# Two model blocks on one core: the first products of each wide norm on unscaled input, latent norms earlier

## What is computed

```
def rmsnorm(x, g):
    xf = x.astype(jnp.float32)
    y = xf * lax.rsqrt(jnp.mean(xf * xf, axis=-1, keepdims=True) + EPS)
    return (y * g.astype(jnp.float32)).astype(x.dtype)

# block 1
hn = rmsnorm(h, mix_norm_g[l]);  proj = hn @ w_in[l]
q_a, k_a, v_a, cq, ckv, k_pe = jnp.split(proj, IN_SPLITS, axis=-1)
#   q, k, v: windowed attention, 8 heads; cq, ckv (512 and 256 columns) are
#   normed again ("latent norms") and go through w_q_up and w_kv_up
h = h + mix @ w_out[l]
h = h + conv_glu(rmsnorm(h, ffn_norm_g[l]), w_gate[l], w_up[l], ...)
#   conv_glu: (silu(conv3(x @ w_gate)) * (x @ w_up)) @ w_down

# block 2; mod = silu(c) @ w_ada + b_ada gives shift, scale and gate of both norms
h = rmsnorm_2(x, norm_mix_g[l]) * (1.0 + sc_m) + sh_m;  proj = h @ w_in[l]
#   a recurrence (hgrn) and a convolution, gated sum "merged"
x = x + gt_m * (merged @ w_o[l])
h2 = rmsnorm_2(x, norm_ffn_g[l]) * (1.0 + sc_f) + sh_f
ff = (silu(h2 @ w_ffn_gate[l]) * (h2 @ w_ffn_up[l])) @ w_ffn_down[l]
x = x + gt_f * ff;  return rmsnorm_2(x, norm_final_g)
```

## Time and profile before

| | before |
|---|---|
| median of 3 runs | 2782.65 us (2779.78 to 2783.17) |
| the profiled execution | 2776.33 us, span 2775.0 us |
| mean granted clock of TensorE | 0.985 of full speed |
| PE busy / DVE busy / ACT busy / POOL busy | 97% / 65% / 44% / 12% of the span |
| moved by DMA | 571 MB, mean 206 GB/s |

### The profile page before, as it was taken

How to read it: one execution, slowest core, us unless ns; L and a number is a source line. 1 busy time by engine, 2 the same in 40 slices (tenths; PEclk the granted TensorE clock), 3 DMA queues, 4 the chain that set the end, 5 groups by cost and what they waited for, 6 DMA issues and landing times. The chain is left out here.

```text
span 2775.0 us, 51102 instructions
## 1 busy us (share of the span) xinstructions
PE 2682.7 (97%) x22036; PEld 2638.7 (95%) x22036; DVE 1800.6 (65%) x2489; ACT 1214.8 (44%) x1861; POOL 321.6 (12%) x533
## 2 busy tenths in 40 slices
PE   7899989899999999998999999999899999999998
PEld 6888879899999999998999999999899999999997
DVE  5656567877777777775788667767554454444454
ACT  4456544544433444434444443334444443344442
POOL 1110113211111111221000001111100000000001
PEclk9999999999999999999999999999999999999999
DMA  6343457688888787885444568887545555555553
GB/s 198 119 118 91 125 178 230 216 266 272 271 280 284 267 274 267 273 275 175 152 152 148 180 224 275 270 278 244 166 164 186 188 181 184 194 192 187 182 186 118
DMA packets 500001, 571.18 MB, mean 206 GB/s; under 512 B 26688, under 2 KB 473280, under 8 KB 499776
## 3 DMA queue, kind: packets, MB, share of 16 engines
q1 hardware_dynamic: 467968, 463.76, 51.2%
q0 software_dynamic: 31520, 103.36, 11.4%
q10 hardware_dynamic: 288, 0.80, 0.1%
HBM read 565.77 MB, written 2.54 MB: 205 GB/s over the span
## 5 line engine op out<-in xcount | busy, mean ns | idle before, releaser
L1596 DVE TENSOR_TENSOR wl<-raw,wh 128x1024 fp32r<-128x1024 f32 (+1 forms) x894 | 1060.3, 1204 | 675.3 <-ACT wh L1143 669.8
L575 PE MATMUL ps<-xx,wh 128*128 128x256 f32 (+2 forms) x5104 | 1459.2, 286 | 39.3 <-DVE xx L1651 18.1
L576 PE MATMUL ps<-xx,wh 128*128 128x256 f32 (+2 forms) x5104 | 1439.1, 282 | 0.0
L577 PE MATMUL ps<-xx,wl 128*128 128x256 f32 (+2 forms) x5104 | 1435.7, 281 | 0.0
L1143 ACT ACTIVATE wh<-raw 128x1024 fp32r<-128x1024 f32 (+1 forms) x894 | 880.9, 1029 | 639.0 <-PE ps L577 631.3
L575 PEld LDWEIGHTS ps<-xx,wh 128*128 128x128 f32 x5104 | 967.2, 190 | 49.4 <-issue 30.2
L576 PEld LDWEIGHTS ps<-xx,wh 128*128 128x128 f32 x5104 | 968.4, 190 | 1.7 <-issue 1.0
L577 PEld LDWEIGHTS ps<-xx,wl 128*128 128x128 f32 x5104 | 967.7, 190 | 0.0
L575 PE MATMUL ps<-hid,wh 128*128 128x256 f32 x1408 | 394.0, 280 | 0.0
L576 PE MATMUL ps<-hid,wh 128*128 128x256 f32 x1408 | 393.6, 280 | 0.0
L577 PE MATMUL ps<-hid,wl 128*128 128x256 f32 x1408 | 392.8, 279 | 0.0
(11 more groups left out here) (300 smaller groups left out, 1949.4 us busy)
## 6 DMA issues: line engine op xcount, KB each, us to landing
raw<-in_w_in SPq DMA_DIRECT2D x118, 1024.0 KB, 5.2
ada_raw<-in_w_ada POOLq DMA_DIRECT2D x384, 256.0 KB, 4.8
raw<-in_w_gate SPq DMA_DIRECT2D x44, 1024.0 KB, 6.7
raw<-in_w_up SPq DMA_DIRECT2D x44, 1024.0 KB, 7.1
raw<-in_w_ffn_gate SPq DMA_DIRECT2D x44, 1024.0 KB, 5.0
raw<-in_w_ffn_up SPq DMA_DIRECT2D x44, 1024.0 KB, 5.1
raw<-in_w_down SPq DMA_DIRECT2D x32, 1024.0 KB, 6.7
raw<-in_w_ffn_down SPq DMA_DIRECT2D x32, 1024.0 KB, 5.5
```

Of the source, the lines that this page charges most:

```text
L575: pe.matmul(dst, h[:, c, o:o + w], x[:, 0, k, g.t0:g.t1], start=(k == 0), stop=False)
L576: pe.matmul(dst, h[:, c, o:o + w], x[:, 1, k, g.t0:g.t1], start=False, stop=False)
L577: m = pe.matmul(dst, l[:, c, o:o + w], x[:, 0, k, g.t0:g.t1], start=False, stop=end)
L1596: dve.tensor_tensor(wl[i % NS][:, part], raw[i % NR][:, part], wh[i % NS][:, part].bitcast(F32), ALU.subtract).then_inc(s_lo, 1)
```

## The change

Each wide norm (`N_IN`, `N_FFN1`, `N_MIX2`, `N_FFN2`) gets a raw operand: chunk times norm gain, without `rstd`, in two parts (ACT `raw_his`, DVE `raw_lows`), made two chunks behind the residuals of the products before. The first two products after the norm (`RAW_KEY`, `RAW_KEY2`) run on it (`gemm_raw`), with the sums of squares inside the first; `rstd` multiplies their results as they are read from PSUM (`unscaled`). The norm itself is a lane paced by ticks, for the third product on. In block 2 the shift is carried as two more columns of the product and added afterwards (`keep_shift`, `shift_of`). The hold is gone. `ada` pauses in these two products and from `merged` to the second `wo` product, and begins four steps later.

At the start SP loads the first part of `H`, slab 0, then the rest; the squares' sums of `N_IN` are POOL's alone; the constants come in two loads. The latent norms start one product earlier, beside `kpe`, and their steps are spread. In the final norm ACT multiplies by the gain beforehand, DVE multiplies 12 chunks in three instructions and POOL four.

```diff
+RAW_LAG = {N_FFN1: {g: ([2 * g - 2, 2 * g - 1] if g < 7 else [12, 13, 14, 15]) for g in range(1, 8)},
+           N_MIX2: {g: ([2 * g - 2, 2 * g - 1] if g < 7 else [12, 13, 14, 15]) for g in range(1, 8)},
+           N_FFN2: {5: [0, 1, 2, 3, 4, 5], 6: [6, 7, 8, 9, 10, 11], 7: [12, 13, 14, 15]}}
+SUMS_AT = {N_IN: 12, N_FFN1: 8, N_MIX2: 8, N_FFN2: 8}
+ROOT_AT = {N_IN: 7, N_FFN1: 5, N_MIX2: 5, N_FFN2: 5}
+SCALE_AT = {N_IN: 8, N_FFN1: 8, N_MIX2: 9, N_FFN2: 6}
 def sync_program(sp):
-            for i in range(4):
-                sp.dma_start(H[:, 4 * i:4 * i + 4, :], hT[:, 4 * i:4 * i + 4, :]).then_inc(s_h[i], 16)
-            sp.wait_ge(s_h[1], 16)
+            sp.dma_start(H[:, 0:4, :], hT[:, 0:4, :]).then_inc(s_h[0], 16)
+                if i == 0:
+                    for q in range(1, 4):
+                        sp.dma_start(H[:, 4 * q:4 * q + 4, :], hT[:, 4 * q:4 * q + 4, :]).then_inc(s_h[q], 16)
 def tensor_program(pe):
+            def gemm_raw(n, key, sums=None):
...
+                for i in g.slabs:
...
+                    for c in range(nk):
+                        k = k0 + c
...
+                        if sums is not None and k == SUMS_AT[n]:
+                            sums(n)
+                        pe.wait_ge(s_rl, raw_base(n) + k + 1)
...
+                        elif sums is None and k in RAW_SHARED[n]:
+                            m.then_inc(s_passed, 1)
+                        if c in ticks(nk):
+                            lanes.pump(c == nk - 1 or c == nk // 2 - 1)
-            pair_sums(N_IN)
-            x_in = normed(N_IN)
-            gemm(("cq", 0), x_in)
-            gemm(("cq", 1))
-            gemm(("ckv", 0))
+            gemm_raw(N_IN, ("cq", 0), pair_sums)
+            gemm_raw(N_IN, ("cq", 1))
+            gemm(("ckv", 0), normed(N_IN))
+            lanes.start("latent", latent())
             gemm(("kpe", 0))
-            lanes.start("latent", latent())
...
+                        if f == 0 and g == 0:
+                            lanes.stop("ada")
+                            gemm_raw(n, (b, "gate", f, g), square_sums)
+                            gemm_raw(n, (b, "up", f, g))
+                            lanes.resume("ada")
+                            continue
-            square_sums(N_FFN1)
             ffn(1)
-            square_sums(N_MIX2)
...
                 if len(gs) == 2:
+                    lanes.stop("ada")
                     lanes.start("merged", pause(12), slow=True, front=True)
...
-                gemm(("wo", g), merged_ready if g == 0 else None, hold=(g == 7))
+                gemm(("wo", g), merged_ready if g == 0 else None)
+                if g == 1:
+                    lanes.resume("ada")
 def gpsimd_program(pool):
+            def first_pairs():
+                bufs = pair_bufs(N_IN)
+                for i in range(KD // 2):
+                    c = norm_src(N_IN, 2 * i + 1)
+                    pool.wait_ge(s_h[(2 * i + 1) // 4], 16)
+                    pool.tensor_tensor(bufs[i][1][:, :], c, c, ALU.mult).then_inc(s_pm, 1)
+                    if i:
+                        add_pair(i - 1)
+                add_pair(KD // 2 - 1)
 def scalar_program(act):
+            def raw_his(n, chunks):
+                for i in chunks:
+                    act.activation(raw_body(n, 0, i), raw_src(n, i), ACT.Copy, scale=norm_gain(n, i)).then_inc(s_rh, 1)
...
                 for j in range(2):
                     squares(N_FFN1, 2 * g + j, H[:, 2 * g + j, 14:T], *last_use(("outa", g), j))
+                raw_his(N_FFN1, RAW_LAG[N_FFN1].get(g, []))
 def vector_program(dve):
+            def raw_lows(n, chunks):
+                for i in chunks:
+                    dve.wait_ge(s_rh, raw_base(n) + i + 1)
+                    dve.scalar_tensor_tensor(out=raw_body(n, 1, i), in0=raw_src(n, i), scalar=norm_gain(n, i), in1=raw_body(n, 0, i).bitcast(F32),
+                                             op0=ALU.mult, op1=ALU.subtract).then_inc(s_rl, 1)
...
-            split(halves[0] + 2)
-            reciprocal(N_FFN1)
-            emit(norm_scales(N_FFN1))
+            lanes.start("norm", norm_scales(N_FFN1), front=True)
             ffn(1)
...
-            for c in range(KD):
-                if c % 4 != 1:
-                    x = H[:, c, 16:T]
...
+            for q in range(3):
+                x = H[:, 4 * q:4 * q + 4, 16:T]
+                dve.wait_ge(s_fa, 4 * q + 4)
+                dve.tensor_tensor(x, x, rstd[:, 0:SEQ].unsqueeze(1).to_broadcast([P, 4, SEQ]), ALU.mult).then_inc(s_fd, 1)
```

More of the change, by code:

```diff
@@ L444, in done, with raw_half, raw_body, raw_src @@
             return GEMMS[key].done
+        def raw_half(n, h, i):
+            if n == N_IN:
+                return raw_in[:, h, i, :]
+            if n == N_FFN2:
+                return raw_ffn[:, h, i, :]
+            return xb[:, h, i, :] if n == N_FFN1 and i < 8 else xx[:, h, i, :]
+        def raw_body(n, h, i):
+            return raw_half(n, h, i)[:, RAW_T1[n] - (T - NORM_T0[n]):RAW_T1[n]]
+        def raw_src(n, i):
+            return H[:, i, NORM_T0[n]:T]
+        def raw_shift(n, h):
+            return xx[:, h, :, Q0:META] if n == N_MIX2 else raw_ffn[:, h, :, 0:META - Q0]
+        def shift_cols(n):
+            return mod[:, 0:16] if n == N_MIX2 else mod[:, 48:64]
+        def raw_base(n):
+            return KD * RAW_NORMS.index(n)
+        def shared_free(n, i):
+            g = GEMMS[RAW_KEY2[n]]
+            if i % 8 == 7:
+                return s_slab, g.slabs[i // 8] + 1
+            before = sum(len([c for c in RAW_SHARED[m] if c % 8 != 7]) for m in RAW_NORMS[:RAW_NORMS.index(n)])
+            return s_passed, before + len([c for c in RAW_SHARED[n] if c % 8 != 7 and c <= i])
+        def shift_of(j):
+            return small[:, 160 + j:161 + j]
         def last_use(key, j):
@@ L579, in gemm @@
                                 m.then_inc(s_slab, 1)
-                        if c in ticks(nk) and not (hold and last):
+                        if c in ticks(nk):
                             lanes.pump(c == nk - 1 or c == nk // 2 - 1)
@@ L799, in tensor_program @@
             for g in range(8):
-                gemm(("outa", g), normed(N_A) if g == 0 else None, hold=(g == 7))
+                gemm(("outa", g), normed(N_A) if g == 0 else None)
             def ffn(b):
@@ L1120, in gpsimd_program @@
                     mod_until(20)
-            emit(norm_lows(N_FFN2))
-            mod_until(24)
+            lanes.start("norm", norm_lows(N_FFN2), front=True)
             ffn(2)
-            for q in range(4):
-                x = H[:, 4 * q + 1, 16:T]
-                pool.wait_ge(s_rr, 9)
-                pool.wait_ge(*last_use((2, "down", 1, 2 * q), 1))
+            pool.wait_ge(s_rr, 9)
+            for c in range(12, KD):
+                x = H[:, c, 16:T]
+                pool.wait_ge(s_fa, c + 1)
                 pool.tensor_tensor(x, x, rstd[:, 0:SEQ], ALU.mult).then_inc(s_fp, 1)
@@ L1144, in split, with gemm @@
                     halves[0] += 1
-            def gemm(key, hold=False):
+            def gemm(key):
                 for i in GEMMS[key].slabs:
                     nk = SLABS[i][3]
-                    held = hold and i == GEMMS[key].slabs[-1]
-                    split(2 * (i + 1) if held else 2 * (i + 2) + 1)
+                    split(2 * (i + 2) + 1)
                     for c in range(nk):
-                        if held:
-                            continue
                         if c in ticks(nk):
@@ L1352, in scalar_program @@
             pair_squares(N_IN)
-            split(1)
             act.wait_ge(s_cst, 16)
-            root(N_IN)
-            emit(norm_his(N_IN, 0))
-            for g in range(2):
-                gemm(("cq", g))
-                for j in range(2):
-                    evac(("cq", g), j, P, cq[:, 2 * g + j, Q0:T])
+            lanes.start("norm", norm_his(N_IN, 0))
+            gemm(("cq", 0))
+            gemm(("cq", 1))
             gemm(("ckv", 0))
@@ L1457, in ffn @@
                     for g in range(8):
-                        gemm((b, "down", f, g), hold=(f == 1 and g == 7))
+                        gemm((b, "down", f, g))
                         for j in range(2):
@@ L2134, in vector_program @@
                     gain_of(1, "ffn2_g", 20)
-            split(halves[0] + 2)
-            reciprocal(N_FFN2)
-            dve.wait_ge(s_gain, 4)
-            emit(norm_scales(N_FFN2))
-            mod_until(24)
+                    dve.wait_ge(s_gain, 4)
+                if g == 5:
+                    raw_shift_lo(N_FFN2)
+                raw_lows(N_FFN2, RAW_LAG[N_FFN2].get(g, []))
+            lanes.start("norm", norm_scales(N_FFN2), front=True)
             ffn(2)
```

373 lines of the change are left out of this document (270 added, 103 removed).

## The result

The changed kernel takes **2759.64 us** (median of 4 runs, 2758.14 to 2762.90), beside it the kernel before 2781.24 (4 runs): a ratio of 0.993, 95% interval 0.9918 to 0.9942. The gain is 21.6 us where 63.7 were forecast, and the time lies above the range of 2703 to 2738. The profiled execution took 2758.96 us, its span 2757.6 against 2775.0.

What follows compares the result with a forecast made beforehand. The prediction saw TensorE gapless in undisturbed products, with time lost to waits and slow clock around the norms; gains of 9.5 + 8.5 + 8 + 15 + 16.5 + 4.7 + 1.5 = 63.7 us gave 2719 us, range 2703 to 2738.

Steps and rivals of the forecast that it cites:

- start (end of the first product): First product `cq` 0: slab 0 loaded earlier, first matmul at 13.9, end at 33.7; gain 9.5 us, bounds 5 and 12.
- latent norms (to the end of `na` 0, 0): Window 72.67 to 95.86: beginning beside `kpe` removes waits and slow clock; gain 8.5 us, bounds 4 and 9.6.
- feed-forward 1: `outa`, gate, up: Products around this norm lose waits and slow clock, less 3 us for DVE falling behind; gain 8 us, bounds 3 and 11.2.
- `N_MIX2`: last `down`, `q`, `f`: Products around the second norm lose their excess, less sums and two added columns; gain 15 us, bounds 12 and 15.5.
- `N_FFN2`: last `wo`, gate, up: Products around the third norm lose their excess, raw low parts hidden; gain 16.5 us, bounds 13 and 17.
- `ada` in `wo` 1 and 2: Stopping `ada` at `merged` removes PE's wait for `ada_acc` in `wo`; gain 4.7 us, bounds 2.5 and 5.2.
- end: Final norm: one four-chunk DVE multiply releases the first output transfer at 1.3 us; gain 1.5 us, bounds 0 and 3.
- Rival A: DVE's backlog exceeds the lookahead in `outa`, gate and up; feed-forward 1 gives 3; total 52, 2731 us; chance 0.15.
- The change void: First two products still wait, by a PSUM bank freed only after `rstd`; about 2765 us; chance 0.03.
- Rival B: Slab 0 lands no earlier, or POOL's sums come late; start gains 3 instead of 9.5; 2726 us; chance 0.12.
- Rival D: `ada` runs out of products, its missing steps run with PE standing; the slower side, 2797 us; chance 0.01.
- Rival C: POOL's squares exclude DVE at the start, up to 13 us of DVE time; start gives 1; 2728 us; chance 0.05.

Runs made afterwards that it cites:

- split ahead: Changed kernel, but while a norm lane runs ACT splits both halves of a slab ahead of the norm pieces: 2747.05 us, 0.988.
- the pace: Kernel with both slab halves split ahead on ACT, plus the 16-chunk norm lane spread over 8 pauses instead of 12: 2738.77 us, 0.9859.
- fastest kernel: Kernel with all four edits, plus the norm lane begun two steps earlier for `N_FFN1`, one for `N_MIX2`: 2725.58 us, 0.9804.
- `ada` at rest: Kernel with slab halves split ahead and quicker lane pace, plus `ada` resting beside the third products of both feed-forwards too: 2735.05 us, 0.9844.
- lane earlier: Kernel with all four edits, plus `SCALE_AT` 6 instead of 8 for `N_FFN1` and 8 instead of 9 for `N_MIX2`: 2725.58 us, 0.9804.
- lighter lane: Kernel of `ada` at rest, with DVE's scales and low parts of `N_FFN1` and `N_MIX2` made for the first 64 columns only: 2728.20 us, 0.9809.
- all four edits: Changed kernel plus slab halves split ahead, quicker lane pace, `ada` resting beside third products, and first-norm squares made by ACT: 2731.32 us, 0.982.
- still quicker pace: Kernel with all four edits, with lane pauses 0, 0, 0, 1 instead of 0, 1, 0, 1 over four chunks: 2728.27 us, 0.9813.
- squares on ACT: Changed kernel, but ACT makes all 16 squares of the first norm and POOL only adds the pairs: 2757.49 us, 0.9921.
- POOL-late run: Changed kernel, but POOL begins the first norm's pair squares only after DVE's sixteen raw low parts: 2763.91 us, 0.9944.
- no-lead run: Changed kernel with the `ada` lane beginning at its old step (`ADA_LEAD` 1 instead of 5): 2769.04 us, 0.9961.

## Why the prediction was wrong

Its own steps against the profiled executions (span 2775.0 to 2757.6, a gain of 17.4), forecast and measured:

| step | forecast | measured |
|---|---|---|
| start (end of the first product) | 9.5 | 4.2 |
| latent norms (to the end of `na` 0, 0) | 8.5 | 0.2 |
| `outb` | 0 | 7.4 |
| feed-forward 1: `outa`, gate, up | 8 | 11.0 |
| `N_MIX2`: last `down`, `q`, `f` | 15 | 14.6 |
| `N_FFN2`: last `wo`, gate, up | 16.5 | 16.6 |
| third and fourth products of these three norms | 0 | -43.6 |
| `ada` in `wo` 1 and 2 | 4.7 | 5.2 |
| end | 1.5 | 1.2 |

The rows add up to 16.8; the other 0.6 us lie scattered over 200 products.

**The step that failed** is the one that has no line in the sum: "A product begun without waiting saves both." The prediction costed what the change takes off the first two products, and its three terms for them came out at 42.2 us against 39.5. It did not cost the norm that those two products go without. That norm is still made, 16 scales and 8 low parts on DVE, 16 high parts on ACT, and the third product reads it at once. The forecast put this at nothing; the three third products gave back 41.5 us. The price was laid on DVE for feed-forward 1 alone, and there on the first two products: 3 us were taken off for a DVE that falls behind in `outa` by nearly 8 us. They gave 11.0 us all the same, close to the bound without any loss (11.2), and the 9.6 us of scales and low parts were paid for one product later. For the other norms the text says that "DVE is half free behind the other norms" and stops. The third product stands only among the things that would prove it wrong. The 43.6 us are 14.4, 14.4 and 12.7 for the third products and 2.1 for the fourth ones. Clock is part of it as it was before: 0.73 to 0.80 in these windows. In feed-forward 2's it is 1.00 up to 2021 us and 0.50 from 2027 to 2033; TensorE was busy for 3.35 us of the 6 before 2021 and for 1.95 of the 6 after.

Why it costs so much, the runs show in three parts, in the order in which the edits were added (another order could divide them otherwise). Order on ACT is worth 11.6 us of the three windows (split ahead), the pace a further 7.8 (63.8 to 56.0), an earlier lane and `ada`'s rest 6.8 more (49.2). What is left in the fastest kernel is 15.2 us over clean products. No run splits it further, but DVE's work for the norm has a share in such excess: without three quarters of its columns in two lanes, two windows fell from 40.0 to 32.0 in an otherwise equal kernel. A busy share of 66 to 74% thus hid two limits, first a pair of engines that wait in turn, then the length of DVE's own pieces; whether the latter counts by DVE's total load or by each chunk's delay stays open.

**Rival A** (DVE becomes the bound) had the right engine and the wrong place: it put it in `outa` and the first two products, where TensorE lost 1.1 us in seven `outa` products and nothing else. In kind it was the nearest of the rivals, and its 2731 us is still 29 us short of the measured time. **The change void** rival was wrong, since the first products did begin on time; that its 2765 us lies nearest is chance. **Rival B** fell: slab 0 was there early. **Rival D** fell: in the kernel after TensorE waited for `ada_acc` once, for 0.9 us; with further rest not at all in three runs (`ada` at rest, lane earlier, lighter lane), once for 1.2 us with all four edits, and once for 0.5 at the still quicker pace.

**Rival C** (POOL's squares hold DVE up) came in, with 5.3 of its 8.5 us: the start gave 4.2 instead of 9.5. The prediction weighed one row, 0.26 us for a split beside a POOL addition, and put 4 us on it, mostly before DVE is needed. The raw low parts took 0.84 us beside POOL and 0.42 without (10.03 and 5.04 us for twelve), so 5.0 us in all, and slow clock on top. With the squares on ACT the product ended at 32.65, so the start term's own working (33.7) was right to 1 us but for this. The Trainium skill, SBUF — State Buffer, Who interferes with whom, has VectorE with two SBUF inputs contend with a GpSimd instruction that reads SBUF, under an exclusive lock. The trace agrees in kind; in size the loss is less than the sum of both lengths: POOL's 0.64 and 0.75 alone plus 0.42 would make 1.1 us a pair, and 0.84 was measured. A nearer row was in the trace before, at the start, where DVE scaled chunks with and without POOL's low part beside it:

```profile
24.13 0.91 DVE L1668 SCALAR_TENSOR_TENSOR sqt<-H,vec,rstd 128x272 f32<-128x272 f32 x2
...
25.31 1.00 DVE L1668 SCALAR_TENSOR_TENSOR nx<-H,vec,rstd 128x272 f32<-128x272 f32 x1
...
30.79 0.49 DVE L1668 SCALAR_TENSOR_TENSOR nx<-H,vec,rstd 128x272 f32<-128x272 f32 x1
...
25.17 0.84 POOL L938 TENSOR_TENSOR xx<-sqt,xx 128x272 fp32r<-128x272 f32 x1 [2.64 <-ACT xx L1227]
```

0.49 us becomes 1.00, by a POOL operation of 0.84, for an operation of the raw low part's kind and size. A split of 1024 columns was the wrong neighbour to read the price from.

**Latent norms.** Window 72.67 to 95.86 did shrink, from 23.2 to 16.45 us, 6.7 against the forecast 8.5; `ckv`, the third product of the first norm, took 5.7 of it back, and `kpe` 0.9. It is the same omission as above, and the edits that help the other third products bring `ckv` back too. The 6.7 is not sharp: that window lasts 14.9 to 18.0 us in the other runs made from the kernel after. **`outb`**: the lead of the `ada` lane was read as lost steps for rival D, not as DVE time freed beside the last heads of attention, on whose softmax TensorE waits in `outb`. **Second and third norm** up to their third product, **`ada`** and the **end** were right within 0.5 us. For `ada` the cause is only half that of the forecast: of its 5.2 us, the 4.0 in `wo` 1 come by the lead without any rest as well as by the rest without the lead.

## What to carry to other kernels

When a product is let go without waiting for its operand, follow the operand: it is still made, and the next reader is one product away. Ask of each queue what stands in front of the late piece. Count a round trip between two in-order engines by its period (here 3.8 us for work that needs 2.8), not by either engine's busy share. Contention is read from the row with the same operation and size, and here it was mended by giving the work to an engine outside the pair, while delaying it only moved the wait. Take the small parts of a change out one by one: here one constant was worth about half of the gain.

## What the runs showed of the hardware that was not expected

DVE and POOL slow each other both ways: raw low parts 0.42 to 0.84 us and 1024-column splits 1.15 to 1.65 beside POOL, POOL's 0.64 and 0.75 us operations 1.62 and 1.74 beside splits (POOL-late run). ACT at the same time was untouched: a square took 0.41 to 0.42 us and two high parts 0.92, with POOL at work (kernel after) and without (POOL late). The attention part varies by up to 3 us between traces of kernels that are the same there: `na` 0, 1 is 17.5 us long in the kernel after and 20.6 in the no-lead run, whose programs differ only once `ada` begins, near 390 us. That is more than the squares on ACT bring. What sets it is not shown.
